# A decoder layer's first piece in two transfers, a halved product in its head, and its last squares in two parts

## What is computed

```python
for l in range(DEPTH):
    h = rmsnorm(x, g_mix[l])
    proj = h @ w_in[l]
    ...
    x = x + (gate_a * y_a + gate_b * y_b) @ w_out[l]
    x = x + cross_attention(rmsnorm(x, g_cross[l]), rmsnorm(mem, g_mem[l]), w_xq[l], w_xkv[l], w_xo[l])
    u = rmsnorm(x, g_mlp[l]) @ w_up[l]
    x = x + jnp.square(jax.nn.relu(u)) @ w_down[l]
return rmsnorm(x, g_final)
```

## Time and profile before

| what | value |
|---|---|
| three runs | 409.03, 409.08 and 410.19 us, median 409.08 us |
| the profiled execution | 410.13 us |
| its span (first to last instruction) | 408.2 us |
| TensorE busy | 400.7 us, 98% of the span |
| TensorE weight loads | 370.8 us, 91% |
| VectorE, ScalarE, GpSimd busy | 331.7 us (81%), 253.6 us (62%), 28.8 us (7%) |
| chain that ended last, TensorE's share | 97% |
| mean granted TensorE clock | 0.996 of full speed |

### The profile page before, as it was taken

One profiled execution on the slowest core, in us unless ns is written; L12 is line 12 of the kernel. 1 busy time (PEld: TensorE's weight loads), 2 busy tenths in 40 slices (PEclk: granted clock), 3 DMA queues, 4 the chain that ended last, 5 costly groups with the idle time before them and its releaser, 6 DMA issues.

```text
span 408.2 us, 7054 instructions
## 1 busy us (share of the span) xinstructions
PE 400.7 (98%) x2863; PEld 370.8 (91%) x2863; DVE 331.7 (81%) x416; ACT 253.6 (62%) x302; POOL 28.8 (7%) x41
## 2 busy tenths in 40 slices
PE   8999999999999999999999999999999999999994
PEld 8999978999999999889998899999999999999983
DVE  5869666977765736884958989999999999999976
ACT  7664337874665634460546757777777777777774
POOL 0089000000000000000110000000000000000022
PEclk9999999999999999999999999999999999999998
DMA  8999554534325265555552235556555555566002
GB/s 317 417 416 395 209 206 147 185 126 165 112 96 206 104 207 199 184 174 180 192 208 103 103 126 198 206 206 209 204 201 211 204 206 210 204 210 244 2 0 104
DMA packets 12539, 77.47 MB, mean 190 GB/s; under 512 B 1376, under 2 KB 1376, under 8 KB 4192
## 3 DMA queue, kind: packets, MB, share of 16 engines
q1 hardware_dynamic: 12224, 76.44, 50.9%
q10 hardware_dynamic: 288, 0.66, 0.4%
HBM read 76.04 MB, written 1.05 MB: 189 GB/s over the span
## 4 chain that ended last, share of the span: by engine, by line
PE 97%; DMA 1%; issue 1%; ACT 1%; POOL 0%; DVE 0%; POOLq 0%; ACTq 0%; DVEq 0%
PE bank L1203 39%; PE bank L1533 18%; PE bank L1228 16%; PE bank L1351 11%; PE bank L1261 3%; PE bank L1363 1%; PE bank L1510 1%; PE bank L1244 1%; DMA head_all<-in_front_dram 1%; PE bank L1477 1%; PE bank L1457 1%; PE bank L1553 1%; PE bank L1404 1%; PE bank L1389 0%; PE bank L1470 0%
## 5 line engine op out<-in xcount | busy, mean ns | idle before, releaser
L747 DVE TENSOR_TENSOR w_lo<-raw,w_hi 128x2048 fp32r<-128x2048 f32 (+2 forms) x69 | 143.0, 2080 | 22.1 <-ACT w_hi L483 21.8
L1203 PE MATMUL bank<-hT_hi,w_hi 128*128 128x256 f32 (+1 forms) x369 | 101.9, 277 | 0.0
L1203 PE MATMUL bank<-hT_lo,w_hi 128*128 128x256 f32 x368 | 101.9, 277 | 0.0
L1203 PE MATMUL bank<-hT_hi,w_lo 128*128 128x256 f32 x368 | 101.8, 277 | 0.0
L483 ACT ACTIVATE w_hi<-raw 128x2048 fp32r<-128x2048 f32 x32 | 61.0, 1916 | 27.4 <-PE bank L1203 14.3
L1203 PEld LDWEIGHTS bank<-hT_hi,w_hi 128*128 128x128 f32 x369 | 69.3, 188 | 0.0
L1203 PEld LDWEIGHTS bank<-hT_lo,w_hi 128*128 128x128 f32 x368 | 69.1, 188 | 0.0
L1203 PEld LDWEIGHTS bank<-hT_hi,w_lo 128*128 128x128 f32 x368 | 69.1, 188 | 0.0
L1351 PE MATMUL bank<-hT_hi,w_hi 128*128 128x256 f32 x128 | 35.6, 278 | 0.0
L1351 PE MATMUL bank<-hT_lo,w_hi 128*128 128x256 f32 x128 | 35.4, 277 | 0.0
L1351 PE MATMUL bank<-hT_hi,w_lo 128*128 128x256 f32 x128 | 35.4, 277 | 0.0
(11 more groups left out here) (219 smaller groups left out, 879.6 us busy)
## 6 DMA issues: line engine op xcount, KB each, us to landing
raw<-in_weights_dram SPq DMA_DIRECT2D x64, 1024.0 KB, 4.8
raw<-in_front_dram SPq DMA_DIRECT2D x4, 512.0 KB, 9.2
head_all<-in_front_dram SPq DMA_DIRECT2D x5, 384.0 KB, 6.3
res<-in_x_dram SPq DMA_DIRECT2D x2, 512.0 KB, 12.8
mem_tok<-in_mem_dram SPq DMA_DIRECT2D x1, 1024.0 KB, 11.9
memT_raw<-in_memT_dram SPq DMA_DIRECT2D x1, 1024.0 KB, 11.0
out_dram<-xs SPq DMA_DIRECT2D x4, 256.0 KB, 2.1
gfin<-in_g_final_dram SPq DMA_DIRECT2D x1, 512.0 KB, 5.8
```

The source lines that it names most:

```text
L747: return nc.vector.tensor_tensor(dst, whole, high.bitcast(fp32), sub)
L1203: last = mm(outs[m][:, tok], w, v[:, k0 + k, tok], start=first and n == 0 and not t, stop=k == nk - 1 and n == 2, skip_group_check=bool(kt ...
```

## The change

1. The activations and gains of k-tile 0 are a piece of their own (288 columns) and stay first on SyncE's queue. The weights of k-tile 0 (256 columns) are the first transfer on ScalarE's queue, with a semaphore of their own, `first_w_in`. Behind it ScalarE's queue now takes the pair. K-tiles 1 and 2, which it took before, go to SyncE's queue.
2. The first product of k-tile 4 in the head (chunk 0, high by high) is issued as two matmuls on 128 tokens each. The halved product of chunk 3 stays.
3. At the end, the last 512 columns of the second token tile are squared in two parts of 256. DVE reports the first of them one step earlier, by `x3_ready`. POOL adds the first two sums and the epsilon into `x3_part`, and DVE adds only the last sum to that.

```diff
-    FRONT = [2 * SEQ + GAINS, 2 * SEQ, 2 * SEQ] + (KT - FIRST) * [3 * SEQ] + 4 * [CH // 2]
-
-
-    ACT_PIECES = (1, 3)
+    FRONT = [SEQ + GAINS, SEQ, 2 * SEQ, 2 * SEQ] + (KT - FIRST) * [3 * SEQ] + 4 * [CH // 2]
...
             for j in range(HEAD_PIECES):
-                dst = piece(j) if j else head_all[:, HEAD - 2 * SEQ:HEAD + GAINS]
-                if j not in ACT_PIECES:
-                    sp.dma_start(dst, front_piece(j)).then_inc(head_arrived[j], 16)
+                dst = piece(j) if j else head_all[:, HEAD - SEQ:HEAD + GAINS]
+                if j != PAIR:
+                    sp.dma_start(dst, front_piece(j + 1 if j else 0)).then_inc(head_arrived[j], 16)
...
+            pool.wait_ge(sumsq_act, 5)
+            nc.gpsimd.tensor_scalar(x3_part[:, :], x3_ms[:, 1, 1:2], x3_ms[:, 1, 0:1], EPS, ALU.add, ALU.add)\
+                .then_inc(x3_part_made, 1)
             x3_rstd(1)
...
-            for j in ACT_PIECES:
-                act.dma_start(piece(j), front_piece(j)).then_inc(head_arrived[j], 16)
+            act.dma_start(head_all[:, HEAD - 2 * SEQ:HEAD - SEQ], front_piece(1)).then_inc(first_w_in, 16)
+            act.dma_start(piece(PAIR), front_piece(PAIR + 1)).then_inc(head_arrived[PAIR], 16)
...
+                if k == 0:
+                    act.wait_ge(first_w_in, 16)
                 ready, n = (piece_hi, 1) if k < KT - 1 else (w_hi_ready, 2)
                 copy(w_tile(w_hi, k), w_in_head(k), ACT.Copy).then_inc(ready, n)
...
-            for t in range(TOK):
-                for c in range(2):
-                    act.wait_ge(x3_ready, 2 * t + c + 1)
-                    copy(scratch[:, 2 * t + c, :], res[:, t, 512 * c:512 * c + 512], ACT.Square, scale=D ** -0.5,
-                         accum_out=x3_ms[:, t, c:c + 1]).then_inc(sumsq_act, 1)
+            for i, (t, c, a, e) in enumerate(((0, 0, 0, 512), (0, 1, 512, 1024), (1, 0, 0, 512), (1, 1, 512, 768),
+                                              (1, 2, 768, 1024))):
+                act.wait_ge(x3_ready, i + 1)
+                copy(scratch[:, 2 * t + a // 512, a % 512:a % 512 + e - a], res[:, t, a:e], ACT.Square,
+                     scale=D ** -0.5, accum_out=x3_ms[:, t, c:c + 1]).then_inc(sumsq_act, 1)
...
-            add_p(1, 1, bank[P3][:, :], r2).then_inc(v_made, 1)
+            add_p(1, 1, bank[P3][:, :], r2).then_inc(x3_ready, 1)
             dve.wait_ge(w_used, LAST + 1)
-            dve.wait_ge(v_made, 6)
+            dve.wait_ge(x3_ready, 4)
...
-            dve.wait_ge(sumsq_act, 5)
-            nc.vector.tensor_scalar(var[:, X3, 1:2], x3_ms[:, 1, 1:2], x3_ms[:, 1, 0:1], EPS, ALU.add, ALU.add)\
-                .then_inc(x3_var, 1)
-            dve.wait_ge(x3_ready, 4)
+            dve.wait_ge(x3_part_made, 1)
+            dve.wait_ge(sumsq_act, 6)
+            nc.vector.tensor_scalar(var[:, X3, 1:2], x3_ms[:, 1, 2:3], x3_part[:, :], None, ALU.add).then_inc(x3_var, 1)
+            dve.wait_ge(x3_ready, 5)
...
+            HALVED = 4
+
...
                         for m in range(2):
                             a = k * SEQ + m * P
-                            i = mm(halves(c)[m], wt[:, c, a:a + P], v[:, k, :],
-                                   start=k == 0 and m == 0 and wt is w_hi and v is hT_hi,
-                                   stop=last and wt is w_lo, skip_group_check=True)
+                            first = wt is w_hi and v is hT_hi and m == 0
+                            for t in (range(TOK) if first and (c, k) == (0, HALVED) else (None,)):
+                                tok = slice(0, SEQ) if t is None else slice(t * P, t * P + P)
+                                i = mm(halves(c)[m][:, tok], wt[:, c, a:a + P], v[:, k, tok], start=first and k == 0,
+                                       stop=last and wt is w_lo, skip_group_check=True)
```

More of the change, by code:

```diff
@@ L240, in x_in_head @@
         def x_in_head(k):
-            return piece(piece_of(k))[:, 0:SEQ]
+            return piece(piece_of(k))[:, 0:SEQ] if k else head_all[:, HEAD - SEQ:HEAD]
         def w_in_head(k):
-            return piece(piece_of(k))[:, SEQ:].rearrange("p (c n) -> p c n", n=SEQ)
+            t = piece(piece_of(k))[:, SEQ:] if k else head_all[:, HEAD - 2 * SEQ:HEAD - SEQ]
+            return t.rearrange("p (c n) -> p c n", n=SEQ)
         def w_tile(t, k):
@@ L268, in hybrid_layer @@
         mo_rsum = sb("mo_rsum", [P, 4])
-        x3_ms = sb("x3_ms", [P, TOK, 2])
+        x3_ms = sb("x3_ms", [P, TOK, 3])
+        x3_part = sb("x3_part", [P, 1])
         x_scale = sb("x_scale", [P, 2])
@@ L331, in hybrid_layer @@
         pool_gained, gfin_moved, x3_var = sem("pool_gained"), sem("gfin_moved"), sem("x3_var")
-        v_scaled, v_added = sem("v_scaled"), sem("v_added")
+        v_scaled, v_added, x3_part_made = sem("v_scaled"), sem("v_added"), sem("x3_part_made")
         fin, fin_act = sem("fin"), sem("fin_act")
@@ L1589 @@
     halves = weights[2:4].reshape(2, P, 2, -1).transpose(0, 2, 1, 3)
-    front = [np.concatenate([xT[:, 0], w0[:, 0], gains], axis=1), np.concatenate([xT[:, 1], w0[:, 1]], axis=1),
+    front = [np.concatenate([xT[:, 0], gains], axis=1), w0[:, 0], np.concatenate([xT[:, 1], w0[:, 1]], axis=1),
              w1[:, 0:2], triples, halves]
```

4 lines of the change are left out of this document (2 added, 2 removed).

## The result

| kernel | median | all runs | ratio to before |
|---|---|---|---|
| before | 409.31 us | 409.01 to 410.19 us, 9 runs | |
| the change | 410.39 us | 410.26 to 410.69 us, 9 runs | 1.0022, 95% interval 1.0014 to 1.0031 |

The change makes the kernel **slower**: by 0.9 us of 409 by the ratio, and the two medians lie 1.1 us apart. I had forecast 408.4 us and a range of 407.9 to 409.5 us: the sign is wrong and the range missed. The bound of 0.3% stands just inside the interval (1.0031), so most of it lies in my class "within 0.3%"; but the parts did not do what I said.

What follows compares the result with a forecast made beforehand. TensorE, busy 98% of the span, was taken to bound the kernel. Halved product -0.45, first piece 0 and last squares -0.19 made -0.64 us, from 409.08 to 408.4 us; range 407.9 to 409.5 us.

Steps and rivals of the forecast that it cites:

- within 0.3%: Whole kernel: measured time less than about 1.2 us from no change, between 407.85 and 410.3 us; given 85%.
- The last squares: -0.19 us: At the end: squaring in two parts brings VectorE's root addition from 403.59 to about 403.40 us; bounds 0 and -0.20 us.
- All behind it (the power, the scaling, the stores) moves along: After the root addition: everything up to the stores shifts earlier by the same 0.19 us.
- The halved product: -0.45 us: Head, k-tile 4: it ends the 117.8 ns pace, so 129 products go at 113.5 ns; bounds -0.45 and +0.11 us.
- my two prices: Halved product of k-tile 4: -0.45 us if it ends the long pace, +0.11 us if the pace does not change.
- my first rival: Head: the halved product ends no long pace and only costs 0.11 us, giving 409.0 us; 15%.
- The first piece: 0: Start: TensorE begins earlier but waits again inside k-tile 1, net 0; bounds -0.36 and +0.15 us.
- between 4.94 and 5.13 us: Start: when k-tile 1, side by side with the pair, was to land, 0.64 us behind 4.30 to 4.49 us.
- my sign of being wrong: TensorE's timeline: any wait past 7 us, or a stretch with 113.5 ns today going at 118 ns, would refute the forecast.
- K-tile 1 lands behind the pair or later: Start: each 0.1 us of lateness delays all that follows by 0.1 us; at 5.3 us, 408.7 us; 8%.
- a long stretch that falls into the long pace: Later stretches: 240 products at the long pace cost 1.03 us, 409.5 us; with 168 more, 410.2 us; 8%.
- my base: Starting point of the forecast: the kernel before's median of 409.08 us over three runs.

Runs made afterwards that it cites:

- e16_one_sem: Kernel before plus only the two-part squares, POOL reporting on ScalarE's semaphore so VectorE waits once: 409.37 us, 0.9991.
- e18_change_again: The whole change, unaltered, timed once more in a later job against the kernel before: 410.53 us, 1.0025.
- e4_squares: Kernel before plus only the last squares in two parts, with POOL's addition and VectorE's second wait: 410.36 us, 1.0019.
- e3_halved: Kernel before plus only the halved product of k-tile 4: 409.81 us, 1.0001.
- e2_piece: Kernel before plus only the first piece in two transfers, with its queues: 409.76 us, 1.0005.
- e7_piece_halved: The whole change without the squares (first piece and halved product only), against the kernel before: 409.71 us, 1.0005.
- e17_change_one_sem: The whole change, but POOL reports on ScalarE's semaphore so VectorE waits once; against the kernel before: 409.74 us, 1.0002.
- e13_early_wait: Kernel before plus one long-met VectorE wait, 5 us before the last product's end and off the path: 409.59 us, 0.9997.
- e14_wait_less: Kernel before plus two-part squares, VectorE's two waits before the root addition swapped, two other VectorE waits removed: 410.34 us, 1.0014.
- e12_first_on_sync: Kernel before plus squares without POOL's step (epsilon left out), both first pieces on SyncE's queue, k-tiles 1 and 2 on ScalarE's: 411.06 us, 1.0026.
- e11_change_fixed: The whole change, but squares without POOL's step and its wait, epsilon left out; against the kernel before: 409.68 us, 1.0005.

## Why the prediction was wrong

**"The last squares: -0.19 us"** is the step that failed, and its sign with it. The working up to the root was sound: with one wait the third store comes 0.20 us earlier, and the end of the span 0.18 us. What I left out stands in the diff: `dve.wait_ge(x3_part_made, 1)` is a second wait, so VectorE has an instruction more. I priced what it waits for ("it is there by 403.25 us and hidden") and not the wait. Against `e16_one_sem` it costs, in the change, 0.24 us up to the third store (3.31 against 3.07 us) and 0.30 us behind it (3.37 against 3.07 us), together 0.53 us; in `e18_change_again` 0.69 us and in `e4_squares` 0.87 us, with the same first part (third store at 3.31 us) and a larger second one. So the term was +0.35 to +0.69 us at the end of the span in place of -0.19 us (6.67, 6.83 and 7.01 us against 6.32 us behind L).

The sentence "All behind it (the power, the scaling, the stores) moves along" failed in the same place: the stores at the end are DMA, and my bounds (0 and -0.20 us) allowed for no other transfer there.

**"The halved product: -0.45 us"** has the mechanism right and the size wrong, because the row that it was taken from is not what the kernel usually does. In `e3_halved` and `e18_change_again` the long pace ends at the new halved product, as forecast. But of the 12 profiles whose head has no halved product, that of before included, only four have the long pace. With my two prices the average is (4 x -0.45 + 8 x 0.11) / 12 = -0.08 us, an estimate. In the profile of the change the pace is short from 7.28 us on, before k-tile 4, and there the halved product costs what my first rival said, some 0.1 us. `e3_halved`, at 1.0001, can't tell either from nothing. The hint was in the numbers that I had: the profiled execution lies 1.05 us above the median, and I wrote that "the edits are worth the same in each". A profile that far above the median should have made me ask which of its rows make it so.

The prediction takes the gap of the Trainium skill ("TensorE: Matmul & The Clock Gate", section "Back-to-back issue gap") as its only one. The section gives that formula for a matmul by itself; for a stream of weight loads and matmuls, which this is, it gives 81 ns at 128 columns and 131 ns at 512. That has no second pace either, and it does not fit: the products of 512 columns in line 1533 start 227 ns apart.

**"The first piece: 0"** holds within what can be measured: `e2_piece` 1.0005, `e7_piece_halved` 1.0005, and `e17_change_one_sem` 0.37 us above `e16_one_sem`, the last with the halved product, all lean to the slow side, and none decides. Two of its steps were off in single profiles. TensorE's first product moved by 0.71 us and not by at most 0.36 us: the row of the zeros' matmuls gives a modelled end, 4.89 us, and I took it for a real one; the first product of the change starts at 4.54 us. And k-tile 1, which I had landing "between 4.94 and 5.13 us", did so in `e17_change_one_sem` (4.94 us) and `e2_piece` (5.06 us), but came at 5.46 us in the profile of the change; over the seven profiles that have this piece `hT_hi` of k-tile 1 starts between 4.71 and 5.81 us. A wait of TensorE past 7 us, my sign of being wrong, is in none of these rows, but `e3_halved` and `e18_change_again` have one of 0.6 us at k-tile 2, one with the old order of the pieces and one with the new. The rival "k-tile 1 lands behind the pair or later" is half of what the profile of the change shows: k-tile 1 is late, in at 1.24 + 4.2 = 5.44 us, but still ahead of the pair at 1.24 + 4.4 = 5.64 us. Starting earlier gained little besides: the first products of the change ran 0.21 us apart up to 5.33 us, twice the later distance, which is the lower level of 1.2 GHz. The profile's rows read 1.00 there, but the packed trace's record of the granted clock begins only at 5.41 us, where the distance falls (5.39 us in the profile of before).

**The rivals.** The one that ended slower, a long stretch that falls into the long pace, did not happen: all stretches cost what they did, to 0.01 us. No rival had a price for a wait that is already met. A smaller part of the miss is my base: with more runs the kernel before had medians of 409.6 to 409.8 us in the five jobs and 409.31 us beside the change, where I counted from 409.08 us.

**What adds up.** Measured and forecast lie 2.0 us apart. Of these 0.23 us are the base, 0.54 to 0.88 us the squares (+0.35 to +0.69 in place of -0.19 us), and some 0.4 us the halved product (-0.08 in place of -0.45 us, by the estimate above): 1.1 to 1.5 us. The rest is not assigned.

## What to carry to other kernels

Count the waits of an instruction before you give it a second one: near the end of this kernel a second wait, met long ago, cost 0 or 0.07 us in front of its instruction by the order of the two, up to 0.27 us behind it, and 0.3 us or more by the code load that moved with it. Two producers can report on one semaphore, so that the consumer waits once for the sum. Read the transfers that are not yours, code loads above all, beside the last stores: with one in there, the end came 0.3 to 0.8 us later in seven profiles of seven. And before a saving is priced from one profile, see how far that execution lies from the median: a pace or a landing that changes from run to run is worth its average, not what that profile shows.

## What was not expected of the hardware

- **Two paces, drawn per execution.** The same matmuls go at 113.4 or 117.8 ns, in the same code. A stretch enters the one or the other at its start or after a wait, and a halved product ended the long one in six of six profiles. What draws it stays open.
- **A stand-alone wait moves a code load.** The 8 KB came 1.7 to 2.0 us behind L in 13 profiles without a wait of its own in front of VectorE's root addition, and 2.5 to 3.5 us in the 7 with one. The number of VectorE's instructions does not decide it (`e13_early_wait`, `e14_wait_less`). Why, and for which engine the code is, the traces do not show.
- **The clock's rise.** In `e7_piece_halved` and `e12_first_on_sync` the products stay about 0.21 us apart up to 10.4 us, in the others this lasts up to 7.3 us at most, though the profile's rows read 1.00 throughout. The packed trace's record of the granted clock begins where the distance falls: at 10.46 and 10.35 us in these two, between 4.14 and 7.34 us in the other 18. In the windows of `e7_piece_halved` (us, TensorE busy and instructions, clock, DMA share, GB/s) only the count shows it:

```profile
8.00:10.00 2.00, 2.00 (x11) 1.00 1.03 415
...
12.00:14.00 2.00, 2.00 (x20) 1.00 1.02 410
```

  Both executions had TensorE idle for 0.6 to 0.7 us before or among its first products, and their spans, 410.0 and 409.7 us, are over 1 us above that of before. Such an idle time alone does not decide it: `e11_change_fixed` has 0.61 us too, and its record begins at 4.54 us. For `e12_first_on_sync`, the slowest kernel tried (1.0026), the late rise may be the rule, since its median of 411.06 us is near its profiled execution's 411.64 us; one profile can't show it. For `e7_piece_halved` it is not: its profiled execution was the slowest of twelve (411.89 us against a median of 409.71 us).
- **No version beats the kernel before beyond doubt.** `e16_one_sem`, at 0.9991 (0.9981 to 1.0001), is the best complete one: the new squares with one wait, without the two parts on the head.
